# A delta-rule recurrence on TensorE: products in four quarters of the array, its levels in a loop, its state steps moved

## The chip, the cores and the metric

One core of one Trainium2 chip runs the whole program; the other seven are idle. The metric is the device time of one execution in microseconds. Five engines work side by side: TensorE (matmuls, and the loads of their stationary operands), VectorE, ScalarE, GpSimd, and SyncE, which here only issues DMAs.

## The reference

Two layers of a diffusion block (a bidirectional RWKV-7 recurrence, grouped attention and neighbourhood attention over 256 context and 1024 latent tokens, width 1024), then two layers of a second block. The change touches the recurrence only, six heads of 64 in two directions:

```python
def _rwkv7_step(S, inp):
    r, w, k, v, kk, b = inp
    sa = jnp.einsum('bhvk,bhk->bhv', S, kk)
    S = S * w[:, :, None, :] - sa[..., None] * b[:, :, None, :] + v[..., None] * k[:, :, None, :]
    return S, jnp.einsum('bhvk,bhk->bhv', S, r)
```

run forward and in reverse over the context from zero states, and from their results over the latents. Everything is float32.

## The kernel before, in words

`rwkv_core` (L1600) runs once per layer, 1280 tokens as ten blocks of 128. A block holds two chunks of 64 tokens, chunk `c` on partitions `half[c]` (0 to 63 or 64 to 127). Three groups `g` of two heads, two directions `d`: `q` = 2d + h numbers the four (direction, head) pairs of a group. Inside a chunk the steps are turned into matrices: `grams` (L1728) makes the 64x64 products between tokens; the inverse of a unit triangular 64x64 matrix is then built by doubling, in levels 1 to 5. `TU` holds the inverse so far, as T and its transpose U; a level is, per group,

- W = ML^T T (`level_w`, L1777), with `ML` the gram masked for that level (GpSimd, L2031, all six levels of a block at once), 8 products of 64x64x64;
- a copy to SBUF by ScalarE (L1939);
- D and its transpose (`level_d`, L1792 and L1795), 16 products (8 in level 5, which needs U only);
- the subtraction TU -= D by VectorE (L1968).

All W and D products of chunk c have their stationary operand on rows half[c] and their result on half[c]: a 64x64 product occupies one quarter of the 128x128 array, and these use the two quarters on the diagonal. A float32 product shows as two matmul records and two weight-load records.

The order on TensorE within a block `b` is written out by hand (`block_of`): three `turned` (eight 128x128 transposes each, L1741 and L1744), mixed with three `start_t` (the transpose of the first U, L1752) and three `bv` (L1763); then levels 1 to 5, each W0 W1 D0 W2 D1 D2. After level 1 comes state step 0 of the previous block (`state`, L1854 and L1862), after level 3 state step 1; after levels 2, 3 and 4 the grams of the next block's groups 0, 1 and 2. Then `solve` (L1805) and `outputs` (L1826 to L1838; their products use all four quarters, rows half[c] and results half[h]) in the order S0 S1 O0 S2 O1 O2. VectorE reads the outputs (L1978, L1980), the states (L1988, L1993), masks grams (L1960) and copies half of the transposes (L1999); ScalarE copies the rest (L1914 to L1923, L1943).

The eight banks of PSUM: 0 and 1 grams, 2 and 3 W, start and solve in turn, 4 and 5 D in turn (also beta-V and outputs of group 1), 6 and 7 transposes, states and outputs of groups 0 and 2. TensorE's code is unrolled over all ten blocks; the other four engines run blocks 2 to 7 as a hardware loop of two blocks a turn (`each`, `steps`). SyncE loads block b + 2 when the outputs of block b are read, and then stores the results of block b.

Of the kernel before, what the change touches and what calls it, by code (L numbers as in the profile page):

```python
# [22 lines left out]
ALU = mybir.AluOpType  # L23
# [31 lines left out]
class Signal:  # L55
# [19 lines left out]
    def spent(self, n):  # L75

        self.base += n
# [1521 lines left out]

def rwkv_core(core):  # L1600

# [4 lines left out]
    NW, ND, NA = 7 * NP, 5 * NP, 6  # L1606
    dl_in, v_in = [core.landing(f"rk_d{g}_loaded", per=2) for g in range(NP)], core.landing("rk_v_loaded", per=4)
    stored = core.landing("rk_y_stored", per=2, lead=1)
    zero, cst = core.counter("rk_zero"), core.move("rk_const", 5)
    pg, dg = core.counter("rk_gram"), core.counter("rk_masked", lead=2 * NP)  # L1610
    ptx, atx, dbk = core.counter("rk_turned"), core.counter("rk_turned_out", lead=0), core.counter("rk_bk_out", lead=0)
    pw, aw = core.counter("rk_w"), core.counter("rk_w_out", lead=2)
    pb, ab = core.counter("rk_bv"), core.counter("rk_bv_out")
    pd, dl = core.counter("rk_d"), core.counter("rk_level")
    ml, tu = core.counter("rk_level_masked"), core.counter("rk_u_start")
    pq, dq = core.counter("rk_qmn"), core.counter("rk_qmn_out", lead=2 * NP)
    dgp = core.counter("rk_diag")
    pn, py = core.counter("rk_next"), core.counter("rk_y")
    dh, dy = core.counter("rk_state", lead=4), core.counter("rk_y_out", lead=4)
    with ExitStack() as s:  # L1620
        D = core.sb(s, "rk_in", [P, 2, NP, 2, NA + 1, P])
        VI = core.sb(s, "rk_vin", [P, 2, 2, NP, P])
        ecb = core.sb(s, "rk_ec", [P, 2, 2, NP, 2])
        G = core.sb(s, "rk_g", [P, 2, NP, 2, 2, 6, CH])
        ML = core.sb(s, "rk_ml", [P, 2, NP, 2, 2, NLEV, CH])
        TU = core.sb(s, "rk_tu", [P, 2, NP, 4, 2, CH])
# [4 lines left out]
        MN = core.sb(s, "rk_mn", [P, 2, NP, 4, P])  # L1631
# [9 lines left out]
        half = [slice(0, CH), slice(CH, P)]  # L1641

        def wbank(u, k):
            return bank[2 + (NW * u + k) % 2]

        def dbank(n):
            return bank[4 + (n + 1) % 2]

        def qbank(g, c):
            return bank[(6 if g % 2 == 0 else 4) + c]  # L1650

        def back(b):

            if isinstance(b, int):
                return (CTX // P - 1) - b if b < CTX // P else (NB + CTX // P - 1) - b
            return (NB + CTX // P - 1) - b

        def each(eng, body):

            n = CTX // P  # L1660
            for b in range(n):
                body(b, b % 2, True)
            steps(eng, NB - n - 2, lambda j, u: body(j + n, u, True), 2)
            for b in (NB - 2, NB - 1):
                body(b, b % 2, b < NB - 1)

        with nc.Block() as block:

            @block.sync
            def _(sp):  # L1670
                for d in range(2):
                    sp.dma_start(mg[:, d, :], T["mask_gram"][d]).then_inc(cst.sem, 16)
                    sp.dma_start(lm[:, d, :, :], T["mask_level"][d]).then_inc(cst.sem, 16)
                sp.dma_start(pair[:], T["pair"]).then_inc(cst.sem, 16)

                def load(b, u):
                    sp.wait_ge(dq.sem, dq.nth(NP * (b - 1)))
                    blk = (b, back(b))
                    for g in range(NP):
                        for d in range(2):  # L1680
                            sp.dma_start(D[:, u, g, d, 0:NA, :], T["CHK"][g * 2 + d, :, :, at(blk[d] * P, P)]
                                         .rearrange("w p t -> p w t")).then_inc(dl_in[g].on(u), 16)
                        if g == 0:
                            for d in range(2):
                                sp.dma_start(VI[:, u, d, :, :], T["VT"][:, at(blk[d] * P, P)]
                                             .rearrange("(g p) t -> p g t", p=P)).then_inc(v_in.on(u), 16)
                                with nc.allow_non_contiguous_dma(reason="two chunks' decays"):
                                    sp.dma_start(ecb[:, u, d, :, :], T["EC"].rearrange("g p d c -> d p g c")
                                                 [d, :, :, at(blk[d] * 2, 2)]).then_inc(v_in.on(u), 16)

                def store(b, u):
                    sp.wait_ge(dy.sem, dy.nth(2 * b + 2))
                    for d, blk in enumerate((b, back(b))):
                        sp.dma_start(T["YR"][d, :, at(blk * P, P)].rearrange("(g p) t -> p g t", p=P), QY[:, u, :, d, 1, :]) \
                            .then_inc(stored.on(u), 16)

                load(0, 0)
                load(1, 1)

                def step(j, u):  # L1700
                    load(j + 2, u)
                    store(j, u)
                n = CTX // P
                for j in range(n):
                    step(j, j % 2)
                steps(sp, NB - 2 - n, lambda j, u: step(j + n, u), 2)
                store(NB - 2, (NB - 2) % 2)
                store(NB - 1, (NB - 1) % 2)
                for u in range(2):
# [1989 lines left out]
```

## Time and profile before

| | us |
|---|---|
| median of 3 runs (lowest, highest) | 4848.48 (4833.61, 4849.16) |
| the profiled execution | 4846.4 |
| its span, first to last instruction | 4844.6 |
| busy: TensorE / weight loads / VectorE / ScalarE / GpSimd | 4227.5 / 3270.1 / 2750.6 / 1536.2 / 1475.2 |
| mean granted TensorE clock, share of full | 0.939 |

Busy time is the union of an engine's instructions. Matmuls are pipelined: the start of a row and that of the next tell the rate, not the lengths. "PEld" is a load of a stationary operand. Idle time carries, in brackets, what ended it; "issue" is time in which the engine waited for nothing that the profile shows.

### The profile page before, as it was taken

How to read it: one execution, taken by the hardware profiler on the slowest of the kernel's cores; microseconds unless marked ns; L12 is line 12 of the kernel's file. 1: busy time of each engine (PE TensorE's matmuls, PEld its weight loads, DVE VectorE, ACT ScalarE, POOL GpSimd, SP SyncE). 2: the span in 40 equal slices, each digit the busy share in tenths (PEclk: the TensorE clock that was granted, in tenths of full speed). 3: DMA queues.
4: the chain of work that ended last, by engine and by line, in shares of the span. 5: the costliest groups of instructions: out<-in, count | busy, mean ns of one | idle time of the engine just before them, and what ended most of it. 6: DMA issues, size and time to landing. Idle time of an engine off the chain costs nothing. (4 is left out here: it accounts for less than half of the span.)

```text
span 4844.6 us, 101734 instructions
## 1 busy us (share of the span) xinstructions
PE 4227.5 (87%) x42066; PEld 3270.1 (68%) x42066; DVE 2750.6 (57%) x4666; ACT 1536.2 (32%) x2721; POOL 1475.2 (30%) x1090
## 2 busy tenths in 40 slices
PE   6999899978999699889995998699788889978898
PEld 4887688845667587678884666478535577854566
DVE  3465445456666457545445665765576657557565
ACT  1333222224552133222222553200255421015542
POOL 2232233302113323323321111565132135523213
PEclk8999899989999899999997999799899999989999
DMA  5455532252225536632324143433403343340325
GB/s 192 150 185 183 153 79 70 71 194 54 59 62 193 155 134 218 201 109 66 75 56 149 45 94 128 166 105 104 139 7 86 91 174 107 108 149 8 81 53 182
DMA packets 517934, 561.29 MB, mean 116 GB/s; under 512 B 112732, under 2 KB 412284, under 8 KB 515380
## 3 DMA queue, kind: packets, MB, share of 16 engines
q1 hardware_dynamic: 389876, 475.93, 31.8%
q10 hardware_dynamic: 127616, 78.95, 5.6%
q8 instruction: 341, 5.59, 0.5%
q14 instruction: 101, 0.83, 0.1%
HBM read 366.75 MB, written 192.23 MB: 115 GB/s over the span
## 5 line engine op out<-in xcount | busy, mean ns | idle before, releaser
L1096 PE MATMUL pr_acc<-hH,pr_wh 128*128 128x512 f32 (+1 forms) x1288 | 482.1, 374 | 0.0
L1097 PE MATMUL pr_acc<-hL,pr_wh 128*128 128x512 f32 (+1 forms) x1288 | 465.8, 362 | 0.0
L1098 PE MATMUL pr_acc<-hH,pr_wl 128*128 128x512 f32 (+1 forms) x1288 | 465.7, 362 | 0.0
L2584 ACT ACTIVATE an_p<-an_p,an_stat 128x1280 f32<-128x1280 f32 (+5 forms) x372 | 339.8, 914 | 163.5 <-DVE an_stat L2662 158.1
L2031 POOL TENSOR_TENSOR rk_ml<-rk_lmask,rk_g 128x384 f32<-128x384 f32 x240 | 232.1, 999 | 462.4 <-DVE rk_g L1960 462.4
L2524 PE MATMUL an_t<-ident,an_p 128*128 128x128 f32 x2152 | 318.8, 282 | 40.5 <-ACT an_pT L2591 28.0
L2617 POOL TENSOR_TENSOR an_kl<-an_k,an_kh 128x1280 fp32r<-128x1280 f32 (+3 forms) x36 | 78.5, 2180 | 894.8 <-DVE an_qh L2642 894.8
L2524 PEld LDWEIGHTS an_t<-ident,an_p 128*128 128x128 f32 x2152 | 235.9, 141 | 164.2 <-issue 68.0
L2658 DVE CUSTOM_DVE_ANT_0 an_p<-an_s,an_mask 128x256 f32<-128x256 f32 (+8 forms) x308 | 275.0, 893 | 100.0 <-PE an_s L2507 67.0
L1968 DVE TENSOR_TENSOR rk_tu<-rk_tu,rk_ps 128x512 f32<-128x512 f32 x300 | 190.5, 635 | 235.3 <-PE rk_ps L1795 235.3
L1465 POOL TENSOR_TENSOR sp_sl<-sp_w,sp_sh 128x512 fp32r<-128x512 f32 x172 | 246.0, 1437 | 197.0 <-DVE sp_sh L1540 178.5
L2549 PE MATMUL an_oacc<-an_pT,an_v 128*64 128x512 f32 (+3 forms) x1224 | 298.0, 561 | 4.5 <-DVE an_pT L2669 1.9
L1374 PE MATMUL sp_acc<-sp_ch,sp_sh 128*128 128x512 f32 x728 | 285.6, 392 | 7.6 <-POOL sp_sl L1465 7.6
L1140 POOL TENSOR_TENSOR pr_wl<-pr_w,pr_wh 128x1024 fp32r<-128x1024 f32 x58 | 143.3, 2471 | 469.9 <-DVE pr_wh L1160 469.9
L1375 PE MATMUL sp_acc<-sp_cl,sp_sh 128*128 128x512 f32 x728 | 285.1, 392 | 0.0
L1376 PE MATMUL sp_acc<-sp_ch,sp_sl 128*128 128x512 f32 x728 | 285.0, 391 | 0.0
L1096 PEld LDWEIGHTS pr_acc<-hH,pr_wh 128*128 128x128 f32 x1288 | 245.3, 190 | 57.7 <-issue 20.5
L2591 ACT COPY an_pT<-an_t 128x512 f32<-128x512 f32 (+3 forms) x356 | 186.0, 540 | 294.5 <-PE an_t L2524 293.6
L1795 PE MATMUL rk_ps<-rk_tu,rk_ws 64*64 64x64 f32 x4800 | 277.0, 219 | 2.7 <-issue 2.5
L1097 PEld LDWEIGHTS pr_acc<-hL,pr_wh 128*128 128x128 f32 x1288 | 245.2, 190 | 37.9 <-issue 0.8
L1098 PEld LDWEIGHTS pr_acc<-hH,pr_wl 128*128 128x128 f32 x1288 | 244.6, 190 | 38.2
L2669 DVE COPY an_pT<-an_t 128x512 f32<-128x512 f32 (+3 forms) x256 | 155.7, 616 | 177.8 <-PE an_t L2524 175.3
(380 smaller groups left out, 10118.8 us busy)
## 6 DMA issues: line engine op xcount, KB each, us to landing
CHK<-ri_out SPq DMA_DIRECT2D x24, 1920.0 KB, 8.0
rk_in<-CHK SPq DMA_DIRECT2D x120, 384.0 KB, 5.8
pr_w<-in_w_in ACTq DMA_DIRECT2D x58, 512.0 KB, 4.3
UT<-pr_out SPq DMA_DIRECT2D x45, 640.0 KB, 4.4
sp_w<-in_w_in ACTq DMA_DIRECT2D x50, 512.0 KB, 5.2
U<-sp_c SPq DMA_DIRECT2D x100, 256.0 KB, 2.0
mod_w<-in_w_mod SPq DMA_DIRECT2D x16, 1024.0 KB, 8.0
mo_w<-in_w_out SPq DMA_DIRECT2D x16, 1024.0 KB, 9.8
```

Source lines behind the costliest of these rows:

```text
L1096: nc.tensor.matmul(out, wh[:, u, k, 0:m], hi, start=(k == 0), stop=False)
L1097: nc.tensor.matmul(out, wh[:, u, k, 0:m], lo, start=False, stop=False)
L1098: ins = nc.tensor.matmul(out, wl[:, u, k, 0:m], hi, start=False, stop=(k == KT - 1))
L1374: nc.tensor.matmul(to, sH[:, a, k, :], cH[:, i, k, :], start=(k == 0), stop=False)
L1375: nc.tensor.matmul(to, sH[:, a, k, :], cL[:, i, k, :], start=False, stop=False)
L1376: ins = nc.tensor.matmul(to, sL[:, a, k, :], cH[:, i, k, :], start=False, stop=(k == H - 1))
L1465: g.tensor_tensor(sL[:, slot(q, i)], weight(q, i), sH[:, slot(q, i)], ALU.subtract).then_inc(w_lo.sem, 1)
L1795: ins = nc.tensor.matmul(o[half[c], q, 1, :], Ws[half[c], g, q, :], TU[half[c], u, g, q, 1, :], start=True, stop=True)
L2524: ins = nc.tensor.transpose(bank[:, j * P:(j + 1) * P], Pm[:, n % NPM, j, col:col + P], ident[:])
L2549: ins = nc.tensor.matmul(O[half * HD:(half + 1) * HD, cs], V[:, c % 2, blocks[n][k], :], PT[:, buffer(n, k), cs], start=(p == 0), stop=(p ...
L2584: nc.scalar.activation(row, row, ACT.Exp, bias=stat[:, n % NPM, j, 1:2], scale=heads[groups[n][0]].scale, accum_out=total[:, n % 4, j:j + ...
L2658: V_.tensor_tensor_reduce(out=Pm[:, n % NPM, j, 0:width], in0=scores_at(m, width), in1=extra, scale=1.0, scalar=-3.0e38, op0=ALU.add, op1= ...
```

## The change

Everything is in `rwkv_core`.

1. `TU` becomes `[P, NP, 2, 4, CH]`, indexed by chunk c: T_c lies on half[1 - c], U_c on half[c]. Grams for the masked matrix go to half[1 - c] (three sets of 8 products instead of two), W contracts over the far half, and D's two products of a chunk go to half[1 - c] and half[c]. `start_t` makes 16 products (the transpose, and a copy of U to the other half).
2. D has three pairs of banks, one per group: (4,5), (6,7), (0,1). W has bank 2, 3, 2. Transposes, starts, grams, outputs and states take pairs too.
3. Levels 1 to 4 are a loop of four turns on TensorE (and only there) whose waits compare with register values; level 5 follows in straight code.
4. Both state steps of block b - 1 stand in the turning phase of block b; the grams of block b + 1 stand after level 4 and inside level 5.
5. GpSimd masks one level of one group at a time (`ML` holds one level), behind the W that used it.
6. VectorE, ScalarE, GpSimd and SyncE are unrolled over the ten blocks; the decays `EC` are loaded once; `MN` is single.

TensorE, the new order and level (old names as above):

```diff
-            ins = nc.tensor.matmul(wbank(u, k)[half[c], q * CH:(q + 1) * CH], ML[half[c], u, g, d, h, lv, :],
-                                   TU[half[c], u, g, q, 0, :], start=True, stop=True)
+    pe.wait_ge(ml.sem, ml.nth(k + 1))
+    pe.wait_ge(dl.sem, dl.nth(k - NP + 1))
+    if not isinstance(lv, int):
+        pe.sem_inc(turn.sem, 1)
+            far = half[1 - c]
+            ins = nc.tensor.matmul(w_at[g][half[c], q * CH:(q + 1) * CH], ML[far, g, d, h, :], TU[far, g, c, q, :],
+                                   start=True, stop=True)
...
+    pe.wait_ge(aw.sem, aw.nth(k + 1))
+    pe.sem_inc(turn.sem, 1)
+    for q in range(4):
+        for c in range(2):
+            nc.tensor.matmul(d_at[g][half[1 - c], c, q, :], TU[half[c], g, c, q, :], Ws[half[c], g, q, :], start=True, stop=True)
+        for c in range(2):
+            ins = nc.tensor.matmul(d_at[g][half[c], c, q, :], Ws[half[c], g, q, :], TU[half[c], g, c, q, :],
+                                   start=True, stop=True)
...
+    turned(b, 0)
+    start_t(b, 0)
+    turned(b, 1)
+    start_t(b, 1)
+    turned(b, 2)
+    start_t(b, 2)
+    if before:
+        state(b - 1, 0)
+    bv(b, 0)
+    bv(b, 1)
+    if before:
+        state(b - 1, 1)
+    bv(b, 2)
+    pe.wait_ge(au.sem, au.nth(NP * b + NP))
+    pe.wait_ge(ab.sem, ab.nth(NP * b + NP))
+    pe.wait_ge(dbk.sem, dbk.nth(NP * b + NP))
+    after(pe, dh, 2 * b)
+    after(pe, dy, 2 * b)
+    with pe.Fori(0, NL - 1) as i:
+        lv = i + 1
+        level_w(b, lv, 0)
+        level_w(b, lv, 1)
+        level_d(b, lv, 0)
+        level_w(b, lv, 2)
+        level_d(b, lv, 1)
+        level_d(b, lv, 2)
+    if more:
+        grams(b + 1, 0)
+    level_w(b, NL, 0)
+    level_w(b, NL, 1)
+    if more:
+        grams(b + 1, 1)
+    last_d(b, 0)
+    level_w(b, NL, 2)
+    last_d(b, 1)
+    if more:
+        grams(b + 1, 2)
+    last_d(b, 2)
```

GpSimd's level mask and SyncE's order:

```diff
+    def level(b, lv, g):
+        k = number(b, lv, g)
+        after(pool, pw, k - NP + 1)
+        masked(ML[:, g], b, g, lv).then_inc(ml.sem, 1)
...
+    for b in range(NB):
+        if b and b + 1 < NB:
+            sp.wait_ge(dq.sem, dq.nth(NP * b))
+            load(b + 1)
+        if b:
+            store(b - 1)
```

## Rows read from the trace of the kernel before

**Rows 1.** The page: span, and busy us of TensorE.

```profile
span 4844.6 us, 101734 instructions
PE 4227.5 (87%) x42066; PEld 3270.1 (68%) x42066; DVE 2750.6 (57%) x4666; ACT 1536.2 (32%) x2721; POOL 1475.2 (30%) x1090
```

**Rows 2.** Busy time by stretch: both recurrences, eight blocks; then clock, DMA share, GB/s.

```profile
560.00:1024.00 464.00, 416.36 (x12740) 393.94 (x12740) 222.36 (x403) 115.84 (x301) 156.89 (x190) 0.97 0.29 73
2100.00:2568.00 468.00, 422.01 (x12739) 398.34 (x12737) 222.26 (x403) 115.48 (x300) 156.87 (x190) 0.96 0.29 72
621.28:976.74 355.46, 325.20 (x10176) 309.31 (x10177) 175.47 (x320) 92.39 (x240) 125.74 (x153) 0.99 0.30 75
```

**Rows 3.** Time line of TensorE: start us, length us, records, idle before.

```profile
621.28 0.41 PE L1741 MATMUL rk_ps<-ident,rk_in 128*128 128x128 f32 x2 [1.59 <-DVE rk_mn L1980]
...
709.43 0.41 PE L1741 MATMUL rk_ps<-ident,rk_in 128*128 128x128 f32 x2 [1.58 <-DVE rk_mn L1980]
...
715.90 1.10 PE L1777 MATMUL rk_ps<-rk_tu,rk_ml 64*64 64x64 f32 x31
...
720.87 0.27 PE L1792 MATMUL rk_ps<-rk_ws,rk_tu 64*64 64x64 f32 x2 [1.28 <-issue]
...
721.80 0.85 PE L1854 MATMUL rk_ps<-rk_h,rk_mn 64*64 64x64 f32 x22
...
723.20 1.15 PE L1777 MATMUL rk_ps<-rk_tu,rk_ml 64*64 64x64 f32 x31
724.34 0.33 PE L1792 MATMUL rk_ps<-rk_ws,rk_tu 64*64 64x64 f32 x4
...
725.32 0.63 PE L1777 MATMUL rk_ps<-rk_tu,rk_ml 64*64 64x64 f32 x16
725.79 0.28 PE L1792 MATMUL rk_ps<-rk_ws,rk_tu 64*64 64x64 f32 x4
...
727.65 1.18 PE L1728 MATMUL rk_ps<-rk_in 64*64 64x128 f32 x29
...
744.44 1.92 PE L1805 MATMUL rk_ps<-rk_x,rk_tu 64*64 64x128 f32 x32
...
754.19 0.41 PE L1741 MATMUL rk_ps<-ident,rk_in 128*128 128x128 f32 x2 [1.56 <-issue]
...
976.74 0.41 PE L1741 MATMUL rk_ps<-ident,rk_in 128*128 128x128 f32 x2 [1.68 <-DVE rk_mn L1980]
```

**Rows 4.** The same time line, outputs of group 0.

```profile
746.45 0.29 PE L1829 MATMUL rk_ps<-rk_g,rk_tx 64*64 64x64 f32 x8
746.57 0.30 PE L1832 MATMUL rk_ps<-rk_g,rk_v 64*64 64x64 f32 x8
```

**Rows 5.** Stretches between TensorE's holes, columns as in rows 2.

```profile
683.71:703.68 19.97, 19.65 (x627) 18.80 (x627) 11.15 (x21) 5.14 (x12) 13.79 (x15) 1.00 0.09 24
703.68:707.38 3.70, 2.40 (x128) 2.26 (x127) 1.49 (x5) 0.00 (x0) 0.00 (x0) 1.00 0.02 4
```

**Rows 6.** The page's DMA queues: packets, MB, share of 16 engines.

```profile
q8 instruction: 341, 5.59, 0.5%
```

**Rows 7.** Time line of ScalarE: first block, then the block of rows 3.

```profile
585.33 0.37 ACT L1919 COPY rk_tu<-rk_ps 128x256 f32<-128x256 f32 x1 [3.38 <-PE rk_ps L1752]
...
589.89 0.84 ACT L1939 COPY rk_ws<-rk_ps 128x256 f32<-128x256 f32 x2
...
716.10 0.37 ACT L1923 COPY rk_x<-rk_ps 128x256 f32<-128x256 f32 x1 [0.37 <-PE rk_ps L1763]
...
723.91 0.84 ACT L1939 COPY rk_ws<-rk_ps 128x256 f32<-128x256 f32 x2 [4.89 <-PE rk_ps L1777]
...
745.53 0.60 ACT L1943 ACTIVATE rk_tx<-rk_ps 128x512 f32<-128x512 f32 x1 [1.66 <-PE rk_ps L1805]
```

**Rows 8.** Time line of VectorE: the first subtraction of level 2.

```profile
725.53 0.69 DVE L1968 TENSOR_TENSOR rk_tu<-rk_tu,rk_ps 128x512 f32<-128x512 f32 x1 [1.53 <-PE rk_ps L1795]
```

**Rows 9.** GpSimd's 256-element additions, 621 to 1000 us: min/median/max ns.

```profile
L2035 POOL TENSOR_TENSOR rk_tu<-rk_ml,rk_pair x24: 725/727/733, 646.0 to 969.6; 128x256 f32<-128x256 f32 x24
```

More of the change, by code:

```diff
@@ L1673, in _ @@
                     sp.dma_start(lm[:, d, :, :], T["mask_level"][d]).then_inc(cst.sem, 16)
[L1674 to L1708, printed above, removed]
+                sp.dma_start(ec[:], T["EC"].rearrange("g p d c -> p g d c")).then_inc(cst.sem, 16)
+                load(1)
+                for b in range(NB):
[4 more added lines that the diff above has]
+                        store(b - 1)
+                store(NB - 1)
                 for u in range(2):
@@ new lines, in start_t, with bv @@
+                            nc.tensor.matmul(start_at[g][far, c, q, :], U0[far, g, q, :], pair[far, :], start=True, stop=True)
+                        for c in range(2):
+                            far = half[1 - c]
+                            ins = nc.tensor.matmul(start_at[g][half[c], c, q, :], pair[far, :], U0[far, g, q, :], start=True, stop=True)
+                    ins.then_inc(pu.sem, 1)
+                def bv(b, g):
+                    u = b % 2
+                    pe.wait_ge(ax.sem, ax.nth(NP * b + g + 1))
+                    if g < 2:
+                        pe.wait_ge(au.sem, au.nth(NP * b + 2))
+                    else:
+                        pe.wait_ge(ab.sem, ab.nth(NP * b + 1))
@@ L1950, in _ @@
-                stored.open(dve)
+                dl.open(dve)
                 nc.vector.memset(H[:, 0], 0.0)
@@ new lines, in level @@
+                def level(b, lv, g):
+                    dve.wait_ge(pd.sem, pd.nth(number(b, lv, g) + 1))
+                    if lv < NL:
+                        o = TU[:, g, :, :, :]
+                        nc.vector.tensor_tensor(o, o, d_at[g], ALU.subtract).then_inc(dl.sem, 1)
+                    else:
+                        for c in range(2):
+                            o = TU[half[c], g, c, :, :]
+                            ins = nc.vector.tensor_tensor(o, o, last_at[g][half[c], 0:256].rearrange("p (q k) -> p q k", k=CH), ALU.subtract)
+                        ins.then_inc(dl.sem, 1)
@@ new lines, in _ @@
+                        turned_beta(b, g)
+                    for i in range(2 if before else 0):
+                        state(b - 1, i)
+                    for lv in range(1, NL):
+                        for g in range(NP):
+                            if lv == 1:
+                                dve.wait_ge(au.sem, au.nth(NP * b + g + 1))
+                            level(b, lv, g)
+                    if more:
+                        masked(b + 1, 0)
+                        masked(b + 1, 1)
@@ L2013, in block_of @@
+                    level(b, NL, 0)
+                    level(b, NL, 1)
+                    if more:
+                        masked(b + 1, 2)
+                    level(b, NL, 2)
                     for g in range(NP):
-                        outputs(b, u, g)
-                for g in range(NP):
-                    masked(0, 0, g)
-                each(dve, block_of)
+                        outputs(b, g)
                 for i in range(2):
-                    state(NB - 1, (NB - 1) % 2, i)
+                    state(NB - 1, i)
@@ new lines, in _ @@
+                for g in range(NP):
+                    level(0, 1, g)
+                for b in range(NB):
+                    for lv in range(2, NLEV):
+                        for g in range(NP):
+                            level(b, lv, g)
+                    diagonals(b)
+                    if b + 1 < NB:
+                        for g in range(NP):
+                            starts(b + 1, g)
+                        for g in range(NP):
+                            level(b + 1, 1, g)
```

464 lines of the change are left out of this document (215 added, 249 removed).

## The prediction

> **What bounds the kernel now.** I read the page first: the span, then the busy shares [rows 1]. TensorE is busy 87% of 4844.6 us, VectorE 57%. The profiled execution took 4846.4 us, 2 us below the median of 4848.48; the sum below is made against 4846.4. Then the stretches [rows 2]: the recurrence runs once per layer, 464 and 468 us, and there the granted clock is 0.97 and 0.96 and TensorE is busy 90%. So 932 us of the span are touched, in 20 blocks (10 a layer).
>
> Then TensorE's time line of one block [rows 3]. Blocks start with the L1741 transposes: 621.28 and 976.74 are eight blocks apart, so a block takes 355.46/8 = 44.4 us; the block followed here takes 754.19 - 709.43 = 44.76. Its parts: turning, starts and beta-V products to 715.90 (6.47); level 1; one state step 721.80 to 723.20 (1.40); level 2, 723.20 to 727.65 (4.45); then grams; levels 3 and 4 with the second state step and two more grams; level 5; from 744.44 solves and outputs, 754.19 - 744.44 - 1.56 = 8.2; 1.56 idle before the next block. In a level, 8 W products take 0.47 us (725.32 to 725.79) and the 16 D products twice that, since L1792 and L1795 alternate, four records (two products) every 0.117. Both use only two of the four 64x64 quarters. Thus 3 x 0.47 + 3 x 0.93 = 4.2 of the 4.45 us are streaming: a level is bound by TensorE.
>
> The outputs use all four quarters, and there 8 records (four products) start every 0.12 us [rows 4]: twice the rate. So four quarters do work side by side in this kernel.
>
> **A second bound: the code.** TensorE's holes named "issue" are not random. Windows laid from hole to hole [rows 5] hold 1254 and 255 matmul and load records: five times and once about 251 (waits come on top). The page's row for the instruction queue says 5.59 MB in 341 packets [rows 6], 16.4 KB each; divided by TensorE's 84,132 records that is about 66 bytes a record, so a packet is about 250 instructions. The hole stands at each packet's edge. In the window 703.68 to 707.38 the records are busy 2.40 us of 3.70 with the DMA share at 0.02: a packet took 3.7 us to come although nothing else was moving, and its fetch began only when the one before was entered: had packets been fetched several ahead, the five slow ones before (19.97 us for five, 4.0 each) would have built a reserve. So straight code runs at most 250 instructions per 3.7 us. A block has 10176/8 = 1272 matmul records and as many loads [rows 2], 10.1 packets, 37.6 us of its 44.4.
>
> **The change, per block.**
> *D in four quarters.* 16 products take 4 x 0.117 = 0.47 instead of 0.93. With three bank pairs no D waits for another group's subtraction. Order W0 W1 D0 W2 D1 D2. The copy starts 0.71 after its W and D0 starts 1.14 after it, at 724.34 [rows 3, 7]; D's start to the subtraction's start is 1.19 now [rows 3, 8], hence 0.72 with D half as long; the subtraction takes 0.69. One group's circle is 1.14 + 0.72 + 0.69 + 0.1 = 2.65. On TensorE: D0 at 1.14, W2 1.61, D1 2.08, D2 at 1.61 + 1.14 = 2.75 to 3.22. That bounds the iteration: 3.3. VectorE's three subtractions (2.07) and ScalarE's three copies (3 x 0.47) hide in it. GpSimd now masks one level at a time behind its W; 256 elements take 0.727 [rows 9], 2.2 per level, ready well ahead of the next W0; free as long as the iteration is over 2.3.
> *Register waits and increments in the loop*: no TensorE row shows one; the looped VectorE and ScalarE show no slower spacing than their unrolled blocks. Bounds: 0, and 0.17 per group (what keeps the level at 4.45, rival C). The nearest row is the looped ScalarE's pair of copies, 0.84 for two of 0.37 [rows 7], so nearly 0: 0.1 per level. A level's pure run is 3.4, four are 13.6.
> *The loop itself.* Body: 3 x (32 + 64) = 288 records plus waits, more than one packet, so it lies in at least two. After the second packet is entered the next packet is fetched over the first; each jump back then finds its target gone. Bounds of a jump back: 0 (all stays) and 7.4 (both packets again). I take one packet, 3.7, three times a block: 11.1.
> The Trainium skill, Runtime: NRT & Kernel Launch, section Instruction fetch mechanics, says that a taken branch whose target is outside the window of two blocks waits for a DMA fetch; by that the trace's one-ahead fetch is the window, and the branch costs what I take. The same section gives TensorE a larger instruction memory, 128 KiB; by that alone the body could stay, which is rival A. No run of before has a TensorE loop.
> *Turning with both state steps.* 6.47 + 2 x 1.40 = 9.27. The loop's entry waits for the last beta-V copy, now seen to end at 716.47, 0.57 after level 1 begins [rows 3, 7]: +0.65. The input DMAs start here as before, so the hole of 1.28 at 720.87 [rows 3] stays: 11.2 in all. State waits for copies of turn 2 or 3, done during the starts. ScalarE's start copy grows from 0.37 to 0.6 (as L1943's 512 elements [rows 7]): hidden by the 1.0 us transposes. Queued behind a late state are bv and the loop; there is 0.1 of slack.
> *Tail.* Grams have 24 instead of 16 products, same columns: 3 x 96 records. Grams + level 5 are 480 records = 1.9 packets x 3.7 = 7.1, over their streaming time (grams 3 x 4 x 0.234, as their columns are twice as many; level 5 6 x 0.47; 2.8 each); grams 0 waits 0.3 for group 1's subtraction (same banks). Solves and outputs, 576 records, 2.25 packets: 8.3. VectorE has two masks ahead of the first last-level subtraction; I count 1.29 each against code that is late anyway. Together 15.7. The 1.56 wait before the next block goes: the transposes use banks freed by the first output.
> *SP, loads, decays.* Loads are issued at the same point (after the previous block's outputs) but first used after the loop, later than now: no stall. Two tiny decay DMAs per direction leave; 0 to -0.3 per block, taken 0. The queue order (load, then store) is unchanged. The other engines are unrolled now; with 320 VectorE and 240 ScalarE records in eight blocks [rows 2] they use up a small part of a packet per block: nothing.
> *First block of each layer.* Now start 2 waits for GpSimd's six-level masks: its copy comes at 585.33 after 3.38 idle, the first W copies at 589.89 [rows 7]; masking level 0 first takes 2 x 0.73 a group. I take 5 us back (between 3.4 and 6).
>
> Sum of a steady block: 11.2 + 13.6 + 11.1 + 15.7 = 51.6, against 44.76: +6.8, 18 times = 122. First blocks: +6.8 - 5, twice: +4. 4846.4 + 126 = 4972; I say **4970 us**. Its own range: 4890 (4750 + 60 jumps x 2.4, part of the fetch hidden behind D2) to 5060 (a quarter of the bodies lie across three packets, some 4 us more per iteration).
>
> **Rivals.**
> *A, the other side: the body stays in instruction memory.* For it: no row says how much code TensorE keeps, only how far ahead it fetches; and the loop takes 864 records per block out of the stream. Against: if there were room for many packets, one-ahead fetching is odd. Then 11.1 goes: 40.5 per block, -4.3 x 18 - 2 x 9 = -95: 4750. It decides at 95/60 = 1.6 us a jump: below that the change is faster. The skill's 128 KiB belongs here.
> *B, both packets come again each time*: the ring keeps only the newest two, and the second (on average 1.7 us of running away) also takes 3.7: +2 per iteration, +6 per block: 4970 + 120 = 5090.
> *C, the loop stays resident but waits against registers and the serial chain W, copy, D, subtract keep a level at about 4.45*: +1.05 x 4 per block: 40.5 + 4.2 = 44.7, the same as now; with the first blocks' 10 us, 4835. For it: 15 semaphore operations per iteration. Against: the looped ScalarE.
> *D not doubled* (the two D products of a chunk share a row group and write two banks): the outputs do just that; under 3%, within B's range.
>
> **Chances.** Forecast 0.44, A 0.34, B 0.14, C 0.08. A measurement of this kernel can tell some 0.3% (15 us) from no change. Faster: A and a third of C, 0.37. Same: the rest of C, 0.05. Slower 0.58. The range reaches from A's value, 4740, to 5110 just beyond B; the likeliest case alone is 4890 to 5060.
>
> **What would show it.** Right: inside the loop, TensorE's holes of about 3.7 us before L-lines of W0 in three of four levels, named issue; D groups of 0.47; the instruction queue at 341 - 20 x 672/250 = 287 packets if the loop stays, at 347 or more (one or two for each of 60 jumps) if it does not. Blocks 51 to 52 us apart. Wrong: no holes at the jump (A, blocks 40 us apart), holes of over 5 us (B), or D groups still 0.93.

## The result, and the profile after

The changed kernel takes 4791.5 us (median of 4 runs, 4789.25 to 4793.78) beside 4843.68 for the kernel before (4 runs, 4833.61 to 4849.16): ratio 0.9894, 95% interval 0.9879 to 0.9909. It is 1.1% faster, where 4970 us, 2.5% above the time given before, was predicted. The profiled execution took 4789.25 us.

The page of the kernel after: span, busy time by engine, and the row of the queue that brings instructions (packets, MB, share).

```profile
span 4787.5 us, 105158 instructions
PE 4137.7 (86%) x43986; PEld 3168.7 (66%) x43986; DVE 2766.8 (58%) x4726; ACT 1548.9 (32%) x2721; POOL 1500.3 (31%) x1210
q8 instruction: 287, 4.70, 0.4%
```

The last row decides the question on which the forecast hung. It was 341 packets [rows 6]; 287 is exactly the number that the prediction worked out for a loop that stays in TensorE's instruction memory (its round 250 instructions a packet helped: with 256 it would have been 288 or 289), and 347 was the least for one that does not. No jump back fetched anything.

A packet is a piece of TensorE's program, some 250 instructions in 16.4 KB; its edge is where the next one is needed. A block is called quick when it takes about 40 us here and slow when it takes about 45. Stretches of the kernel after: three blocks, eight blocks of each layer, then loop and tail of a quick block and the loop of a slow one (the columns of [rows 2]).

```profile
654.65:699.98 45.33, 38.19 (x1375) 35.00 (x1369) 23.14 (x44) 12.19 (x30) 16.85 (x25) 0.96 0.28 72
699.98:740.39 40.41, 36.28 (x1371) 33.59 (x1368) 22.73 (x43) 12.19 (x30) 16.85 (x25) 1.00 0.31 81
740.39:786.17 45.78, 38.51 (x1374) 35.27 (x1368) 22.95 (x44) 12.19 (x30) 16.90 (x25) 0.96 0.26 71
613.92:953.88 339.96, 296.35 (x10949) 272.96 (x10944) 183.09 (x344) 97.50 (x240) 134.94 (x200) 0.98 0.29 77
2127.61:2468.16 340.55, 294.92 (x10950) 271.65 (x10945) 183.19 (x344) 97.49 (x240) 134.96 (x200) 0.99 0.30 77
711.49:727.39 15.90, 14.24 (x576) 12.80 (x577) 7.61 (x12) 4.46 (x12) 9.09 (x14) 1.00 0.17 48
727.39:740.39 13.00, 12.63 (x528) 12.23 (x528) 9.49 (x21) 2.91 (x6) 7.76 (x12) 1.00 0.02 5
752.70:772.29 19.59, 16.00 (x576) 14.42 (x577) 7.52 (x12) 4.46 (x12) 9.14 (x14) 0.91 0.13 36
```

Eight blocks take 339.96 and 340.55 us, 42.5 each; before it was 355.46, 44.4 [rows 2]. Quick and slow blocks alternate: by the start of the first transposes 40.7, 45.3, 40.4, 45.8, 40.0, 44.6, 40.6, 42.5. From first transposes to the start of the last block the first layer went from 399.5 to 377.8 us and the second from 405.0 to 378.5, 48 of the 57 us between the two spans; the rest lies in the last blocks and around the recurrences. TensorE does more in a block, 1369 matmul records for 1272 (a product is two), and is still quicker.

The time line of TensorE in a quick block, then in the slow one behind it (start, length, records, idle before).

```profile
708.51 0.92 PE L1882 MATMUL rk_ps<-rk_h,rk_mn 64*64 64x64 f32 x24 [1.20 <-issue]
711.49 1.15 PE L1803 MATMUL rk_ps<-rk_tu,rk_ml 64*64 64x64 f32 x32 [0.90 <-ACT rk_x L1963]
713.78 0.21 PE L1813 MATMUL rk_ps<-rk_ws,rk_tu 64*64 64x64 f32 x1 [0.41 <-issue]
716.08 1.15 PE L1803 MATMUL rk_ps<-rk_tu,rk_ml 64*64 64x64 f32 x32
717.31 0.27 PE L1813 MATMUL rk_ps<-rk_ws,rk_tu 64*64 64x64 f32 x2
717.80 0.60 PE L1803 MATMUL rk_ps<-rk_tu,rk_ml 64*64 64x64 f32 x14
719.50 0.23 PE L1815 MATMUL rk_ps<-rk_tu,rk_ws 64*64 64x64 f32 x2
719.86 1.15 PE L1803 MATMUL rk_ps<-rk_tu,rk_ml 64*64 64x64 f32 x32
...
752.70 0.24 PE L1803 MATMUL rk_ps<-rk_tu,rk_ml 64*64 64x64 f32 x1 [0.90 <-ACT rk_x L1963]
753.26 1.15 PE L1803 MATMUL rk_ps<-rk_tu,rk_ml 64*64 64x64 f32 x31 [0.33 <-issue]
758.47 0.27 PE L1815 MATMUL rk_ps<-rk_tu,rk_ws 64*64 64x64 f32 x2 [1.81 <-issue]
759.23 1.72 PE L1803 MATMUL rk_ps<-rk_tu,rk_ml 64*64 64x64 f32 x32 [0.20 <-issue]
764.23 1.25 PE L1803 MATMUL rk_ps<-rk_tu,rk_ml 64*64 64x64 f32 x32 [0.26 <-issue]
```

L1803 is the W products, L1813 and L1815 the two halves of D. The quick block's turns begin at 711.49, 716.08 and 719.86: 3.78 us for a turn without a hole. D's 16 products of a group start within 717.31 to 717.80, 0.49 us, where they took 0.93. The last D product starts at 719.50 and the next turn's W at 719.86: a jump back costs some 0.3 us, not 3.7. The slow block has two holes in its first turn, at its second record (753.26) and near its end (758.47), about 256 instructions apart: its body of 300 lies across three packets and two edges are crossed in 5.8 us. The quick block's has one edge (713.78). Behind the hole of 1.81 the granted clock fell:

```profile
759.20:762.00 2.80, 2.77 (x73) 2.72 (x75) 0.74 (x2) 0.74 (x2) 1.45 (x2) 0.64 0.01 3
```

### The profile page after: what moved, and what is told of

Same layout as the page of the kernel before. It is cut to its first block and busy times, and to the rows that moved or that the text cites. A ratio compares the mean times of both kernels' runs of the same rounds, so it can differ in the third digit from the quotient of the medians.

```text
span 4787.5 us, 105158 instructions
## 1 busy us (share of the span) xinstructions
PE 4137.7 (86%) x43986; PEld 3168.7 (66%) x43986; DVE 2766.8 (58%) x4726; ACT 1548.9 (32%) x2721; POOL 1500.3 (31%) x1210
## 5 line engine op out<-in xcount | busy, mean ns | idle before, releaser
L2078 POOL TENSOR_TENSOR rk_ml<-rk_g,rk_lmask 128x256 f32<-128x256 f32 x300 | 213.3, 727 | 410.9 <-PE rk_ps L1803 410.6
L2010 DVE TENSOR_TENSOR rk_tu<-rk_tu,rk_ps 128x512 f32<-128x512 f32 x240 | 164.8, 688 | 198.9 <-PE rk_ps L1815 192.4
L2569 PE MATMUL an_s<-an_kh,an_qh 128*128 128x256 f32 (+2 forms) x564 | 200.0, 367 | 21.5 <-POOL an_qh L2684 13.5
```

Source lines behind the costliest of these rows:

```text
L2078: return nc.gpsimd.tensor_tensor(out, G[:, b % 2, g, :, :, 0, :], lm[:, :, lv:lv + 1, :].to_broadcast([P, 2, 2, CH]), ALU.mult)
```

## The experiments

Each was timed beside the kernel before on the same chip; the ratio to it follows the time, its interval in brackets. The kernel before moves by a few microseconds from one such timing to the next, so where a difference to the changed kernel comes out otherwise by the ratios, both are given.

**1. The levels unrolled on TensorE**, all else as in the changed kernel.

```diff
-                    with pe.Fori(0, NL - 1) as i:
-                        lv = i + 1
+                    for lv in range(1, NL):
...
-                    pe.sem_inc(turn.sem, 1)
```

> The changed kernel with levels 1 to 4 unrolled on TensorE again (waits against constants, no register increments); nothing else differs. Theory S (the loop's body stays in instruction memory, so the loop saves code packets): 861 more instructions per block have to be fetched, 10.8 packets of 256 instead of 7.5; at 3.7 us a packet the code alone takes 40.1 us a block, and with the holes at the input loads a block takes 44 to 46 us instead of 42.5: 4791 + 20 x 2 = 4830 us (4810 to 4860), and the instruction queue carries about 355 packets instead of 287. Theory J (each jump back fetches a packet again, as the forecast had it): 60 jumps go and with them up to 3.7 us each; the time falls, to 4700 or less.

Measured: 4838.6 us, 0.9977 [0.9966, 0.9988]. So the loop alone is worth 47 us (40 by the ratios), and all the rest of the change without it 0.2%. The page's queue row, ScalarE's copies behind the W products, and TensorE's holes:

```profile
q8 instruction: 354, 5.80, 0.5%
```

```profile
728.21 0.84 ACT L1965 COPY rk_ws<-rk_ps 128x256 f32<-128x256 f32 x2 [1.93 <-PE rk_ps L1803]
731.79 0.84 ACT L1965 COPY rk_ws<-rk_ps 128x256 f32<-128x256 f32 x2 [1.59 <-PE rk_ps L1803]
735.96 0.84 ACT L1965 COPY rk_ws<-rk_ps 128x256 f32<-128x256 f32 x2 [2.17 <-PE rk_ps L1803]
740.90 0.84 ACT L1965 COPY rk_ws<-rk_ps 128x256 f32<-128x256 f32 x2 [2.94 <-PE rk_ps L1803]
```

```profile
735.12 0.27 PE L1812 MATMUL rk_ps<-rk_ws,rk_tu 64*64 64x64 f32 x1 [0.60 <-issue]
738.91 0.27 PE L1812 MATMUL rk_ps<-rk_ws,rk_tu 64*64 64x64 f32 x2 [0.52 <-issue]
742.82 0.72 PE L1740 MATMUL rk_ps<-rk_in 64*64 64x128 f32 x25 [1.05 <-issue]
```

A level without a hole takes 3.58 us (728.21 to 731.79), the others 4.2 and 4.9. Holes stand 3.8 and 3.9 us apart, one at each packet: here the block is bound by its code, as the kernel before was. That D in four quarters buys nothing here, since the time turns up as holes, is read from these rows; the unrolled levels were not run with D in two quarters. The pair of turns without a hole also gives the jump's price: 3.78 - 3.58 = 0.20 us a turn.

**2. The loop's first instruction at the start of a packet.**

```diff
-                    with pe.Fori(0, NL - 1) as i:
+                    with nc.Fori(0, NL - 1, engines=[mybir.EngineType.PE], head_slot={mybir.EngineType.PE: 0}) as i:
```

> The changed kernel, but each loop's first instruction is put at slot 0 of a code packet of 256 (the body is 300 instructions, so it now lies in two packets, its edge late in the first turn). In the changed kernel the heads stand at slots that fall by 16 every second block: odd blocks 109 to 45 (two packets, blocks of 40 to 41 us), even blocks 245 to 181 (an edge right behind the head and another 256 later, three packets at the start, blocks of 45 us with a 1.8 us hole and then the clock at 0.64 to 0.68 for 5 us). Theory L (where the edges fall in the first turn, under the input loads, makes the difference between even and odd blocks): all blocks take 40.5 to 41.5, 1.3 us less on average: 4791 - 25 = 4766 us (4750 to 4780), and the mean clock in the recurrences rises. Rival: even and odd blocks differ by something else of their parity (buffers, loads): the alternation 45 / 40.5 stays, 4791 +- 5, or a few us more for the skipped slots.

Measured: 4848.36 us, 1.0003 [0.999, 1.0017], a miss. There are 11 packets more (298), for the padding, and nearly every entry into the loop now waits for the loop's first packet, 3.0 to 4.3 us in nine blocks of the first layer:

```profile
727.08 1.97 PE L1803 MATMUL rk_ps<-rk_tu,rk_ml 64*64 64x64 f32 x32 [3.00 <-issue]
```

Yet one thing was learnt: the alternation went, all blocks of the first layer took 44 to 46 us. This points to where the loop's head lies in its packet: in the compiled program a block's code is seven packets and 120 instructions long, so from block to block the head moves by about half a packet.

**3. The back jump announced to the fetcher.**

```diff
-                    with pe.Fori(0, NL - 1) as i:
+                    with nc.Fori(0, NL - 1, engines=[mybir.EngineType.PE], hint_back_edge=True) as i:
```

> The changed kernel with the loop's jump announced ahead (a hint at the head of each turn that its target is to be fetched). Theory S (the target is in memory anyway): nothing to gain, one more instruction per turn: 4791 to 4797 us. Theory J (jumps fetch again, part of it hidden): 60 jumps get cheaper by up to 3.7 us: 4650 to 4750.

Measured: 4852.87 us, 1.0014 [1.0001, 1.0028], 61 us over the changed kernel; both theories missed it. The packets are still 287. Turns are 3.89 us (727.43, 731.32, 735.21), and the first instruction behind the loop waits:

```profile
742.43 0.55 PE L1740 MATMUL rk_ps<-rk_in 64*64 64x64 f32 x11 [2.55 <-issue]
```

The changed kernel has no hole at that place (727.39). What I read from it, without a run that shows it alone: the hint takes the place of the fetching ahead that otherwise goes on while the loop turns. The instruction queue agrees as far as it goes: in this block it brings nothing from 724 to 740 us, which is nearly the whole loop, and one packet within the changed kernel's loop from 711.5 to 727.4.

**4. D's products chunk by chunk**: the same 16, but neighbours now read the same half of the rows, so at most two quarters are at work at once.

```diff
-                    for q in range(4):
-                        for c in range(2):
+                    for c in range(2):
+                        for q in range(4):
                             nc.tensor.matmul(d_at[g][half[1 - c], c, q, :], TU[half[c], g, c, q, :], Ws[half[c], g, q, :], start=True, stop=True)
-                        for c in range(2):
                             ins = nc.tensor.matmul(d_at[g][half[c], c, q, :], Ws[half[c], g, q, :], TU[half[c], g, c, q, :],
```

> The changed kernel with the 16 products of D in another order: chunk by chunk instead of both chunks in turn, so that neighbours share their 64 rows and at most two quarters can be at work; same products, same result. If the four quarters are what shortens a level (forecast: 0.47 instead of 0.93 per D), a D group takes 0.93 again and a turn of the loop 3.78 + 1.0 = 4.8 us: 80 turns x 1.04 = +83, 4875 us (4850 to 4890). If the order of products does not matter (the array takes them in any order, or a level is bound by copies and subtractions): 4791 +- 5.

Measured: 4819.88 us, 0.9949 [0.993, 0.9967], 28 us over the changed kernel. Copies behind the W products of successive turns:

```profile
720.14 0.84 ACT L1966 COPY rk_ws<-rk_ps 128x256 f32<-128x256 f32 x2 [1.86 <-PE rk_ps L1803]
724.41 0.84 ACT L1966 COPY rk_ws<-rk_ps 128x256 f32<-128x256 f32 x2 [1.90 <-PE rk_ps L1803]
```

A turn is 4.27 in place of 3.78, 80 turns x 0.49 = 39 us, of which 28 reach the end. From its first start to its last a group's D takes 0.76 to 0.82 us, where it is 0.48 to 0.52 in the changed kernel; it stays under the 0.93 of before, as the order lets part of it overlap. Inside the loop, where code is no bound, the four quarters are worth something; this is the other half of experiment 1.

**5. How much code does TensorE keep?** Five loops of four turns ahead of the first recurrence, nothing but small products (the edit is shortened).

```diff
+                for packets in (2, 4, 6, 8, 10) if probe else ():
+                    with pe.Fori(0, 4):
+                        for _ in range(64 * packets - 16):
+                            nc.tensor.matmul(bank[3][:, 0:64], ident[:], ident[:, 0:64], start=True, stop=True)
```

> A measurement of the disputed thing by itself: how much code can TensorE's instruction memory keep for a jump back? Ahead of TensorE's recurrence of the first layer stand five loops of four turns, each body nothing but small fp32 products (128x128 by 64 columns into a bank that is free then), 450, 962, 1474, 1986 and 2498 instructions long, so 2, 4, 6, 8 and 10 packets of 256 instructions. The program grows from 73,711 to 81,096 instructions on TensorE, 317 packets if each is fetched once. If the memory holds only the block in work and the next (the reading on which my forecast stood), every turn of every loop after the first brings its packets again: 3 x (1 to 2 + 3 + 5 + 7 + 9) or more, so 390 to 420 packets in the instruction queue, and holes of about 3.7 us at each jump. If it keeps a wider window behind the jump (S, the body of the levels stays), the small loops run without holes and only those whose body is wider refetch: 317 packets if even 2,500 instructions stay, 317 + 3 x 10 = 347 to 350 if only the last does not, 317 + 3 x 18 = 371 if the last two do not, and so on. The length of each turn beside that of the first tells which loop it is. The time of the whole kernel is longer by the loops themselves and says nothing.

Measured, in one execution: 382 packets. A product takes 0.223 us there (449 of two records each in 100 us), so the loops begin at 565, 665, 880, 1208 and, after the clock's fall, near 1960. Time line, stretches (TensorE's busy time, loads, the other engines' zeros, clock, DMA share, GB/s), and the queue row of 1208 to 1319 and of 1319 to 1536, first and second turn of the fourth loop:

```profile
944.76 260.46 PE L1728 MATMUL rk_ps<-ident 128*128 128x64 f32 x2331
...
1320.36 1.55 PE L1728 MATMUL rk_ps<-ident 128*128 128x64 f32 x6 [1.46 <-issue]
1323.44 6.88 PE L1728 MATMUL rk_ps<-ident 128*128 128x64 f32 x32 [1.54 <-issue]
```

```profile
960.00:1195.00 235.00, 235.00 (x2106) 235.00 (x2106) 0.00 (x0) 0.00 (x0) 0.00 (x0) 1.00 0.00 0
1230.00:1318.00 88.00, 88.00 (x791) 88.00 (x789) 0.00 (x0) 0.00 (x0) 0.00 (x0) 1.00 0.01 1
1340.00:1520.00 180.00, 180.00 (x846) 180.00 (x845) 0.00 (x0) 0.00 (x0) 0.00 (x0) 0.50 0.00 1
```

```profile
q8 instruction: 8, 0.13, 0.5%
...
q8 instruction: 11, 0.18, 0.3%
```

The fifth loop, nearly whole, and the queue row of its first and second turn (1961 to 2224, 2225 to 2490):

```profile
1961.00:3020.00 1059.00, 1059.00 (x4964) 1058.84 (x4965) 0.00 (x0) 0.00 (x0) 0.00 (x0) 0.50 0.00 1
...
q8 instruction: 11, 0.18, 0.3%
...
q8 instruction: 12, 0.20, 0.3%
```

The third loop's body has 1474 instructions. Nothing is fetched from 960 to 1195, nearly all of its last three turns, and TensorE never stops. The fourth's has 1986: it stands 1.46 us at its first jump and 1.54 six records later, 1.72 and 1.21 us at the two jumps that follow, and fetches everything again in each turn. The fifth's has 2498 and is fetched again in each turn too, yet TensorE does not stop once. So at least 1474 instructions stay and 1986 do not; the level loop has 300. And code that has to come again has no fixed price: here it is 3.0, 1.7, 1.2 us and nothing. These products are long, 0.22 us and at the lower clock 0.43, against 0.03 to 0.06 in a level, so what a refetched jump would cost the level loop is not shown. The Trainium skill, Runtime: NRT & Kernel Launch, section Instruction fetch mechanics, gives TensorE 128 KiB or 2048 instructions, and in the same section a window of two blocks of 256. The runs contradict the second, since 1474 stay. They are in accord with the first: 1986 fail a little below that bound, and that fetching ahead takes the rest is my reading.

**6. The loop rotated**, so that the jump falls where TensorE waits for a copy and each wait at the entry stands ahead of its own use (shortened; the waits at the entry are left out).

```diff
+                    level_w(b, 1, 0); level_w(b, 1, 1); level_d(b, 1, 0); level_w(b, 1, 2); level_d(b, 1, 1)
-                    with pe.Fori(0, NL - 1) as i:
+                    with pe.Fori(0, NL - 2) as i:
+                        level_d(b, i + 1, 2)
+                        level_w(b, i + 2, 0); level_w(b, i + 2, 1); level_d(b, i + 2, 0); level_w(b, i + 2, 2); level_d(b, i + 2, 1)
+                    level_d(b, NL - 1, 2)
```

> The loop is rotated. The two first W products, D's first quarter pair, the third W product and the second D group of level 1 stand as straight code ahead of the loop, each behind its own wait only; the loop makes three turns of D's last group of one level and the first parts of the next; the last level's last D group stands behind it. Arithmetic and order are unchanged. TensorE's program grows to 79,589 instructions, 311 packets. S (the loop is free of refetching, what it costs is 0.2 to 0.3 us at each jump and 0.9 us at its entry, where one wait stands for what used to be several): the jump now falls where TensorE waits for a copy anyway and the entry wait is spread, -0.2 x 3 - 0.9 = -1.5 us a block or -30 us in all, against 1.15 packets more of straight code a block, which cost nothing where they are fetched ahead: 4760 to 4775. L (straight code is what costs: each packet edge that falls in the levels or the turning phase opens a hole of 0.5 to 1.3 us, as the unrolled levels showed, 5 edges more for 2.8 us a block): +0.5 to +1.3 for each of 1.15 edges, 12 to 30 us, which eats the gain: 4780 to 4795.

Measured: 4788.99 us, 0.987 [0.9847, 0.9894], no different from the changed kernel. The 0.9 at the entry went, 23 packets came (310), and their edges open holes in the levels, as at 758.00:

```profile
758.00 0.21 PE L1816 MATMUL rk_ps<-rk_tu,rk_ws 64*64 64x64 f32 x1 [1.63 <-issue]
```

**7. The next block's input loads issued behind the first D of level 1**, a phase later.

```diff
                     if b and b + 1 < NB:
                         sp.wait_ge(dq.sem, dq.nth(NP * b))
+                        sp.wait_ge(pd.sem, pd.nth(number(b, 1, 0) + 1))
                         load(b + 1)
```

(The store of the block before now comes ahead of the loads.)

> TensorE's program is untouched. The loads of the next block's inputs are issued only when D of level 1 has its first group, instead of ahead of the levels, so that they don't run beside the packets that TensorE fetches for the turning phase and the loop's first turn. L (the slow blocks, 44.6 to 45.8 beside 40.0 to 40.7, are slow because a packet comes late while input loads hold the DMA engines, and the clock falls after the hole): the holes of 1.8 us at the packet edge go and with them the drop to a granted clock of 0.64 to 0.68, so most blocks come to 40.5: -2 us x 18 = -36, 4755. If only half of the slow blocks are cured, or the loads now hit the packets of the tail instead, 4775 to 4800. S alone, without L (the alternation is the place of the loop's head in its packet, nothing of the loads): no change, 4785 to 4797, with slow blocks where they were. A cost that would show otherwise: inputs come too late for the next turning phase, its first products waiting for a DMA, +1 us or more a block, 4810.

Measured: 4763.92 us, 0.9819 [0.9796, 0.9841], 28 us under the changed kernel (36 by the ratios), and the two intervals do not touch. That the store now goes first was not run by itself.

**8. Both.**

> The rotated loop and the late input loads together. If the two costs are apart from each other, their differences to the changed kernel (4791) add: -30 and -36 give 4725. If the holes of the packet edges are the one cause of both (L), the late loads make the added straight code free and the sum is at least as large as the better of the two alone: 4725 to 4755. If the loads are not it, the time is that of the rotated loop alone.

Measured: 4769.51 us, 0.984 [0.9819, 0.9861]. The rotated loop, which gained nothing alone, gains nothing here either. It wants a packet just when the late loads run. The hole, and the stretch ahead of it (DMA share and GB/s are its last two columns):

```profile
713.54 0.48 PE L1817 MATMUL rk_ps<-rk_tu,rk_ws 64*64 64x64 f32 x3 [4.57 <-issue]
```

```profile
707.00:713.50 6.50, 1.88 (x86) 1.63 (x82) 0.70 (x2) 0.95 (x3) 2.01 (x3) 0.85 1.21 298
```

The longest holes inside a turn, 4.57, 4.57 and 4.11 us in three blocks of the first layer, stand here; the traffic is the input loads'.

**9 and 10. The loads another turn later**, behind the first D of level 2, with the changed kernel's loop and with the rotated one.

```diff
-                        sp.wait_ge(pd.sem, pd.nth(number(b, 1, 0) + 1))
+                        sp.wait_ge(pd.sem, pd.nth(number(b, 2, 0) + 1))
```

> The next block's input loads are issued when D of level 2 has its first group, a turn later than in the kernel with late loads (4763.9). TensorE's program is the changed kernel's. By theory L (a packet that has to be fetched while the loads hold the DMA engines comes late, TensorE stands, and its clock falls for some microseconds) no packet is then wanted while the loads run: the loop's body is complete after its first turn and the loads, some 12 us, end with the loop. The 1.81 us hole in the first turn of every second block (seen with the late loads at 752.99, DMA share above 1 right behind) goes with the clock dip behind it: the slow blocks, 42.8 to 44.9, come to 39 or 40, -3 x 9 = -27: 4735 to 4745. Rival M (those holes come from the loop's body lying across three packets, whatever the loads do): 4760 to 4770, slow blocks still every second one, with 1.8 us holes in the first turn.

> The rotated loop with the loads of the next block issued at D of level 2. With loads at level 1 this kernel (4769.5) has holes of 4.57 us at a packet edge in D of the first level, with a DMA share of 1.21. By L these go (one in every second or third block, 4.6 plus 1 for the clock, some 6 or 7 in all, -35) and the rotated loop keeps its own gain at the entry: 4725 to 4740. By M and by the cost of straight code (a packet edge opens a hole whatever the loads do) it stays at 4760 to 4775.

Measured: 4771.89 us, 0.9851 [0.9834, 0.9867], and 4756.93 us, 0.9826 [0.981, 0.9843]. For the plain loop theory L fell and M held: the slow blocks stay (43.2, 43.0, 44.8) and so does the hole of 1.81. In the rotated one the holes of 4.57 are gone, and nothing over 2.6 us is left in its blocks. Its median is the lowest of all, but by the ratio it is no better than experiment 7, and its interval overlaps that of experiment 8 as well.

**11. The loads in the loop's last turn** (`number(b, 4, 0)`).

> The same with the loads issued at D of level 4, in the loop's last turn, so that they run through the tail, where TensorE needs a packet every 3.6 us. By L the holes move there: three or four packets under loads at 5 us in place of 3.6, +4 to +5 us a block against the loads in the second turn, and the next block's turning phase may wait for its inputs: 4810 to 4840, near the kernel before. By M the place of the loads does not matter: 4760 to 4770.

Measured: 4866.93 us, 1.0052 [1.0035, 1.0069]. The size is beyond what L expected and the mechanism is another: the next block's grams stand right behind the loop and wait for their inputs.

```profile
738.89 1.99 PE L1741 MATMUL rk_ps<-rk_in 64*64 64x64 f32 x48 [3.44 <-DMA rk_in<-CHK]
742.93 1.13 PE L1741 MATMUL rk_ps<-rk_in 64*64 64x64 f32 x48 [0.74 <-DMA rk_in<-CHK]
746.57 0.68 PE L1741 MATMUL rk_ps<-rk_in 64*64 64x64 f32 x24 [0.84 <-DMA rk_in<-CHK]
```

So it says nothing clean of packets under loads. It does show how late is too late: behind the first D of turn 1 or 2 the loads are in time, of turn 4 they are not.

**12. No input traffic to speak of** (shortened; the blocks compute with stale inputs).

```diff
-                            sp.dma_start(D[:, u, g, d, 0:NA, :], T["CHK"][g * 2 + d, :, :, blk[d] * P:(blk[d] + 1) * P]
+                            w, n = (NA, P) if b < 2 else (1, 4)
+                            sp.dma_start(D[:, u, g, d, 0:w, 0:n], T["CHK"][g * 2 + d, 0:w, :, <the stretch it holds>]
```

> A bound for L: the changed kernel with its loads at their old point, but from the third block on each of the six large loads of a block is cut to a sliver (128 x 4 numbers of the same stretch that the buffer already holds), so it leaves out nearly all input traffic of 16 of 20 blocks and computes with stale inputs; instructions, waits and program of TensorE are the same. If what the input loads cost is all in the packets that they delay, this kernel stands where the best placing of the loads stands, 4735 to 4745 (L), blocks at 39 to 40 without alternation. By M 4785 to 4797 as the changed kernel, with the alternation. If even this is above the kernel with loads in the second turn, the loads in the loop cost nothing at all.

Measured: 4767.62 us, 0.9842 [0.9825, 0.9858]. Eight blocks of experiment 12 and of 7, and a hole of 12:

```profile
616.00:940.00 324.00, 289.39 (x10927) 266.95 (x10923) 183.13 (x344) 97.62 (x240) 135.08 (x200) 1.00 0.09 23
```

```profile
616.00:940.00 324.00, 291.48 (x10854) 269.59 (x10853) 181.00 (x339) 97.02 (x239) 133.99 (x199) 0.98 0.31 81
```

```profile
752.56 0.27 PE L1816 MATMUL rk_ps<-rk_tu,rk_ws 64*64 64x64 f32 x2 [1.81 <-issue]
```

Right behind that hole:

```profile
753.00:756.00 3.00, 2.71 (x109) 2.44 (x107) 1.20 (x2) 0.81 (x3) 1.43 (x3) 1.00 0.01 3
```

With a DMA share of 0.09 in place of 0.31 the kernel is no faster than with well placed loads. Input loads cost the changed kernel 24 us by this run (25 by the ratios), and experiment 7, with 28 (36), took all of it. The hole of 1.81 stands at the same place in the turn without loads: L had it wrong, and what is left is M. The first turn crosses two edges in some 5 us when the loop's head lies late in a packet, and in straight code packets come 3.7 us apart. Quick and slow blocks still alternate (38.3 to 39.6 and 41.4 to 43.3 us in the first layer). The clock does not follow the hole, though: behind 1.81 us it was 0.64 in the changed kernel and is 1.00 here, so the hole alone does not bring it down. What else has to be there is open.

## Why the prediction was wrong

**The step that failed** is "after the second packet is entered the next packet is fetched over the first; each jump back then finds its target gone", priced at 3.7 us, three times a block: 11.1. That term alone turned a faster kernel into a slower one. Measured: nothing fetched at a jump (287 packets), 0.20 us a turn (experiment 1) to 0.36 (719.50 to 719.86, start to start). Experiment 5 shows why: at least 1474 instructions stay. Over 18 blocks the term is 200 us, more than the whole miss of 178. The range given, 4740 to 5110, holds 4791.5 only because it was drawn out to rival A's value; the range of the likeliest case, 4890 to 5060, does not. What led me there was a true reading with a false step behind it. The trace of before showed that packets are fetched only a little ahead [rows 5]. I took the distance of fetching ahead for the size of the memory. They are two numbers: old packets stay behind, as the probe's third loop shows. The rival named this ("no row says how much code TensorE keeps, only how far ahead it fetches") and should have had the larger chance, since the case against it was only that one-ahead fetching would be odd.

The price had a flaw of its own. In the window 703.68 to 707.38 of the kernel before, the queue's row is

```profile
q8 instruction: 1, 0.02, 1.8%
```

1.8% of 16 engines over 3.70 us is 1.1 us of transfer. So 3.7 us is how often straight code gets a packet, not how long one is on its way, and it was no price for a single jump; the probe's jumps cost 0 to 3.0 us. What fills the other 2.6 us between packets no run shows.

**Rival A**, 4750 and blocks of 40.5, is what happened: packets exact, no holes at jumps, quick blocks 40.0 to 40.7. Its 41 us shortfall is in the other blocks. By terms, for the two blocks followed (699.98 and 740.39):

- *Turning*: 11.2 forecast, 11.5 and 12.3. Near, and with late loads 10.1 in the quick blocks; the entry's wait for the last beta-V copy is 0.90 (forecast 0.65).
- *Four level turns*: 3.4 each forecast, 13.6. Measured 15.9 and 19.6 with the jumps, 3.78 for a clean turn. D's 0.49 was right (0.47); the third group's D starts 0.2 later than reckoned and the jump adds its 0.2. The first turn is longer, 4.6 us in the quick block and 6.5 in the slow: a fetch inside it. TensorE is also granted less over the slow block's loop, 0.91 against 1.00 over the quick one's. I had given neither a price.
- *Tail*: 15.7 forecast at 3.7 a packet; measured 13.0 and 13.9. It begins with a packet already there: the fetcher works on while the loop turns. In the quick block's loop one packet came, in its tail four.
- *First blocks*: forecast 1.8 us longer than the first block of before (44.0), measured 37.8. Relative to a steady block, the 5 us were nearly right: a first block is now 4.7 shorter (42.5 - 37.8), where it was 0.4 shorter before (44.4 - 44.0), so 4.3 came back.

Forecast 51.6, measured 43.1 for the mean of these two: -10.3 by the jumps, -2.2 by the tail, +0.7 by the turning phase, +3.3 by the turns.

**The second bound was read rightly and is the reason for the gain.** Experiment 1 is the change without the loop: 0.2%. The products saved turn into waits for code. With the loop, 3 of 4 turns take no code, and then the faster D counts as well (28 us, experiment 4). A block's code from loop head to loop head is 1912 instructions in the compiled program, 7.5 packets; 7.5 x 3.7 + 3 turns of 3.78 = 39.1, and 40.0 with the entry's wait. Without input traffic blocks took 40.7 (experiment 12); this estimate leaves 0.7.

**Rival B** (4970 to 5090) falls with the forecast. **Rival C** (turns held at 4.45) was wrong: 3.78. It has a grain of truth, since a turn is longer than 3.4. **D not doubled**: 0.49, wrong.

**Loads.** "Loads are issued at the same point ... no stall" holds for what reads them: nothing waited for an input. They delayed the packets of the turning phase (1.20 at 708.51, which is gone with late loads). The trace of before had such a hole (1.28 at 720.87) that I kept in the sum without tracing it to its cause: 1.28 x 20 = 26 us, near the 24 to 36 that the loads cost by experiments 12 and 7. So the time was in the sum, and the reason was not.

Still open is whether all blocks would take 38 to 40 us if every loop's head lay in mid packet without padding; it was not tried. The hole of 1.2 us that went with the late loads and the 1.81 that stayed look alike in the trace, and I can tell them apart only by experiments 7 and 12.

## What to carry to other kernels

Divide the stretch's time by the instruction queue's packets before pricing products: where TensorE runs straight code at a packet per 3.7 us, as here, fewer or faster products turn up as holes, and a short loop takes its repetitions out of that stream (47 us here). How far an engine fetches ahead does not say how much it keeps; a probe of loops of growing length settles that in one run. Bulk loads are best issued where the engine that streams code is inside a loop and the data are still in time: 28 us gained behind level 1, 75 lost behind level 4.

## What the runs showed of the hardware that was not expected

- TensorE keeps at least 1474 instructions behind a jump and fetches again at 1986. With idle DMA engines its holes there were 3.0 us (in two), 1.7 and 1.2, and none in the loop of 2498.
- In the probe the granted clock was 1.00 for 750 us of products without a pause and fell to 0.50 behind the two holes of 1.5 us (1.2 GHz in place of 2.4), and stayed there for the next 1700 us, though TensorE was busy all the time but for two more such holes. Behind a hole of 1.81 us inside the levels it was 0.64 in the changed kernel and 1.00 where the input loads were cut to slivers.
- A packet that has to come while bulk loads hold the DMA engines (share 1.21, 298 GB/s) made TensorE stand for 4.57 us; the holes inside the turns in experiment 12 were 1.82 at most.
- Telling the fetcher of the back jump cost 61 us, and aligning the loop with its packet 57.
